# When the second pair of gated linear recurrence tiles runs: beside the chunks of the delta-rule recurrence, in buffers of its own

## What is computed

```python
proj = h @ w_in
pa, xb, gb = jnp.split(proj, (A_PROJ, A_PROJ + B_WIDTH), axis=-1)
ya = rwkv7_time_mix(pa, ...)                       # delta-rule recurrence, 8 heads of 64
yb = rglru_mix(xb, gb, ...)                        # gated linear recurrence, 512 channels
return jnp.concatenate([ya, yb], axis=-1) @ w_out

# rglru_mix
xc = conv_b + sum(xp[:, i:i + seqlen] * conv_w[i] for i in range(4))
r = sigmoid(blocks(xc) @ gate_a_w + gate_a_b)
i_g = sigmoid(blocks(xc) @ gate_x_w + gate_x_b)
log_a = -8.0 * r * softplus(-lam)
u = sqrt(-expm1(2.0 * log_a)) * i_g * xc
h_t = exp(log_a)_t * h_(t-1) + u_t
yb = h * gelu(gb)
```

## Time and profile before

| | |
|---|---|
| median of three runs | 3627.5 us (3625.55 to 3630.48) |
| the profiled execution | 3622.88 us |
| its span, first to last instruction | 3621.2 us |
| TensorE busy | 3446.0 us (95%), 20308 matmuls |
| VectorE, ScalarE busy | 1943.7 us (54%), 1330.2 us (37%) |
| granted TensorE clock, mean | 0.973 |
| instruction queue q8 | 160 packets, 2.62 MB |

### The profile page before, as it was taken

How to read it: one execution, slowest core, us unless ns; L and a number is a source line. 1 busy time by engine, 2 the same in 40 slices (tenths; PEclk the granted TensorE clock), 3 DMA queues, 4 the chain that set the end, 5 groups by cost and what they waited for, 6 DMA issues and landing times.

```text
span 3621.2 us, 47103 instructions
## 1 busy us (share of the span) xinstructions
PE 3446.0 (95%) x20308; PEld 2741.7 (76%) x20308; DVE 1943.7 (54%) x2721; ACT 1330.2 (37%) x1958; POOL 4.0 (0%) x18
## 2 busy tenths in 40 slices
PE   8999896799999999989999999999999999989998
PEld 6888665778888788877578887766788877668886
DVE  5554576456553654243445433566766455766644
ACT  4332454133322423233543322244444233544433
POOL 0000000000000000000000000000000000000000
PEclk9999996899999999999999999999999999999999
DMA  5444330014444342222012222310232231012321
GB/s 182 144 140 146 121 111 20 4 65 140 140 145 143 125 137 96 99 79 87 1 53 99 98 95 102 119 59 24 74 107 99 96 137 59 30 57 95 99 99 58
DMA packets 93087, 342.41 MB, mean 95 GB/s; under 512 B 10320, under 2 KB 10960, under 8 KB 92368
## 3 DMA queue, kind: packets, MB, share of 16 engines
q1 hardware_dynamic: 92880, 339.40, 28.1%
HBM read 337.26 MB, written 2.10 MB: 94 GB/s over the span
## 4 chain that ended last, share of the span: by engine, by line
PE 86%; DVE 7%; ACT 5%; issue 1%; DMA 0%; SPq 0%; DVEq 0%; ACTq 0%
PE ps L755 21%; PE ps L756 20%; PE ps L757 20%; PE ps L772 3%; PE ps L773 3%; PE ps L776 3%; PE ps L795 1%; PE ps L796 1%; PE ps L797 1%; PE ps L1127 1%; DVE SPL L1901 1%; PE ps L1137 1%; ACT SPH L1369 1%; ACT WK L1805 1%; DVE WK L2565 1%
## 5 line engine op out<-in xcount | busy, mean ns | idle before, releaser
L1901 DVE TENSOR_TENSOR SPL<-RAW,SPH 128x1024 fp32r<-128x1024 f32 x522 | 636.7, 1224 | 1066.8 <-ACT SPH L1369 1066.7
L755 PE MATMUL ps<-HH,SPH 128*128 128x512 f32 x2352 | 929.4, 395 | 15.7 <-DVE SPL L1901 6.2
L1369 ACT ACTIVATE SPH<-RAW 128x1024 fp32r<-128x1024 f32 x522 | 548.1, 1056 | 1075.1 <-PE ps L757 957.9
L756 PE MATMUL ps<-HL,SPH 128*128 128x512 f32 x2352 | 918.3, 390 | 0.0
L757 PE MATMUL ps<-HH,SPL 128*128 128x512 f32 x2352 | 918.0, 390 | 0.0
L755 PEld LDWEIGHTS ps<-HH,SPH 128*128 128x128 f32 x2352 | 443.3, 188 | 121.3 <-issue 10.5
L756 PEld LDWEIGHTS ps<-HL,SPH 128*128 128x128 f32 x2352 | 443.6, 189 | 94.7 <-issue 4.0
L757 PEld LDWEIGHTS ps<-HH,SPL 128*128 128x128 f32 x2352 | 443.3, 188 | 93.2
L755 PE MATMUL ps<-AH,SPH 128*128 128x512 f32 x1152 | 449.7, 390 | 0.0
L757 PE MATMUL ps<-AH,SPL 128*128 128x512 f32 x1152 | 448.3, 389 | 0.0
L756 PE MATMUL ps<-AL,SPH 128*128 128x512 f32 x1056 | 410.8, 389 | 0.0
(11 more groups left out here) (430 smaller groups left out, 3575.1 us busy)
## 6 DMA issues: line engine op xcount, KB each, us to landing
RAW<-in_ws SPq DMA_DIRECT2D x522, 512.0 KB, 3.3
RAW<-in_wa SPq DMA_DIRECT2D x96, 512.0 KB, 3.3
WK<-in_sm SPq DMA_DIRECT2D x2, 2784.0 KB, 10.5
WK<-in_cst SPq DMA_DIRECT2D x2, 1664.0 KB, 6.8
X<-in_x SPq DMA_DIRECT2D x8, 256.0 KB, 7.9
out<-X SPq DMA_DIRECT2D x8, 256.0 KB, 2.0
WK<-in_sm SPq DMA_DIRECT2D x1, 768.0 KB, 5.4
PCT<-in_pc SPq DMA_DIRECT2D x1, 349.0 KB, 3.0
```

What stands on the lines that cost most here:

```text
L755: e.matmul(out, wh, rhs[0], start=start, stop=False)
L756: e.matmul(out, wh, rhs[1], start=False, stop=False)
L1369: e.activation(SPH[:, q:q + 1024], RAW[:, r:r + 1024], ACT.Copy).then_inc(hi_ready.did(("hi", n)))
L1901: e.tensor_tensor(SPL[:, q:q + 1024], RAW[:, r:r + 1024], SPH[:, q:q + 1024].bitcast(F32), ALU.subtract).then_inc(lo_ready.did(("lo", n)))
```

## The change

Parts 1 to 4 of tiles 2 and 3 leave the first inverse and stand beside chunks 0 and 1, a tile after the other (`LRU_CHUNK_AT`); part 0 stands one step later than before. The two tiles get other buffers: A and M2 in the last tiles of HH and HL, which they share (so tile 3 waits in part 1 for the scan of tile 2), U in tiles of their own. The last results (part 4) of both are taken after tile 3 is done, since they overwrite those buffers. The chunks wait for `("ml", 5)` only.

```diff
 LRU_AT = {0: [(0, 0), (1, 0)], 1: [(0, 1), (1, 1)], 2: [(0, 2), (1, 2)], 3: [(0, 3), (1, 3)],
-          4: [(0, 4), (1, 4), (2, 0), (3, 0)], 5: [(2, 1), (3, 1)], 6: [(2, 2), (3, 2)], 7: [(2, 3), (3, 3)],
-          8: [(2, 4), (3, 4)]}
+          4: [(0, 4), (1, 4)], 5: [(2, 0), (3, 0)]}
+
+LRU_CHUNK_AT = {(0, 1): [(2, 1)], (0, 3): [(2, 2)], (0, 5): [(2, 3)], (0, 6): [(3, 1)], (1, 0): [(3, 2)],
+                (1, 1): [(3, 3)], (1, 3): [(2, 4), (3, 4)]}
...
             if c and 0 < i <= STEPS_NORM:
                 yield "norm", c - 1, i - 1
+            for j, part in LRU_CHUNK_AT.get((c, i), ()):
+                yield "lru", j, part
...
+        YLc, _ = place("YLc", 2 * T, at=h_at + 14 * T * 4)
...
-        lru_places = [{"M2": wk(26), "A": wk(27), "U": wk(12)}, {"M2": wk(28), "A": wk(29), "U": RS[:]}]
+        lru_places = [{"M2": wk(26), "A": wk(27), "U": wk(12)}, {"M2": wk(28), "A": wk(29), "U": RS[:]},
+                      {"M2": YLc[:, T:2 * T], "A": Yh[:, 7 * T:8 * T], "U": YLc[:, 0:T]},
+                      {"M2": YLc[:, T:2 * T], "A": Yh[:, 7 * T:8 * T], "U": Yh[:, 6 * T:7 * T]}]
...
-                        w.wait_ge(("pe0", 14 + j), ("pe0", 21), ("prep_dd",), *([("ml", 2 + j)] if j >= 2 else []))
+                        w.wait_ge(("pe0", 14 + j), ("pe0", 21), ("prep_dd",), ("proj", s, 21))
...
-                        w.wait_ge(("ga", j), ("halved_b",))
+                        w.wait_ge(("ga", j), ("halved_b",), *([("h_", 2)] if j == 3 else []))
...
-                        w.wait_ge(("yb", j), ("proj", s, 21))
+                        w.wait_ge(("yb", 3 if j == 2 else j), ("proj", s, 21))
```

More of the change, by code:

```diff
@@ L588, in plan_mix0 @@
                     chunk(c, i)
+                elif what == "lru":
+                    lru(c, i)
                 else:
@@ L1506, in lru @@
                 def lru(j, part):
-                    L = lru_places[j % 2]
+                    L = lru_places[j]
                     if part == 0:
@@ L1567, in chunk @@
                         for name, dst, done in (("ktp", rwkv["KT"], "kt"), ("btp", rwkv["BT"], "bt")):
-                            w.wait_ge((name, c), ("prep_dd",), *([("yp", c - 1)] if c else [("ml", 7)]))
+                            w.wait_ge((name, c), ("prep_dd",), *([("yp", c - 1)] if c else [("ml", 5)]))
                             e.activation(dst, ps[name, c][:], ACT.Copy).then_inc(act_done.did((done, c)))
@@ L1578, in chunk @@
                     elif i == 6:
-                        w.wait_ge(("yp", c), *([("ylo", c - 2)] if c >= 2 else [("ml", 7)]))
+                        w.wait_ge(("yp", c), *([("ylo", c - 2)] if c >= 2 else [("ml", 5)]))
                         e.activation(rwkv["Y"][c % 2], ps["yp", c][:], ACT.Copy).then_inc(act_done.did(("yc", c)))
@@ L2187, in chunk @@
                         for hf in range(2):
-                            w.wait_ge((name, c), *([("yp", c - 1)] if c else [("ml", 7)]))
+                            w.wait_ge((name, c), *([("yp", c - 1)] if c else [("ml", 5)]))
                             e.tensor_tensor(v4(MX[name, hf]), v4(ps[name, c, hf][:]), bc4(strict if i == 0 else incl),
```

2 lines of the change are left out of this document (1 added, 1 removed).

## The result

| | before | changed |
|---|---|---|
| median, thirteen runs of each | 3627.5 us (3616.6 to 3635.1) | 3619.2 us (3613.9 to 3623.4) |
| ratio changed to before, 95% | | 0.9978 (0.9970 to 0.9987) |
| the profiled execution, its span | 3622.9, 3621.2 us | 3613.9, 3612.2 us |

The changed kernel ran in two more series: 3621.4 against 3626.1 us (0.9989, 0.9979 to 0.9999) and 3622.7 against 3626.7 us (0.9994, 0.9985 to 1.0002). The mean of the three ratios is 0.9987, or **4.7 us faster**; the first series, with 8.3 us, was its best, and in the third the interval takes in no change at all. The forecast was 1.3 us faster. Single runs of one kernel lie up to 18.5 us apart, so this is a case in which the profile's stretches say more than the medians.

A forecast was written before the change was run, and what follows sets the result against it. Instruction fetch, about 3.65 us per 128 small matmuls, was taken to bound the inverse. Terms -4.1 + 0.1 + 0.2 + 0.8 + 1.7 = -1.3 us gave 3626.2 us from the median 3627.5, range 3619 to 3633.

The forecast's parts named there:

- What paces the inverse: First inverse, chunks 0 and 1: instruction fetch sets about 3.65 us per 128 matmuls; moving the work out gains 4.1 us.
- Rival B: First inverse: waits for VectorE and ScalarE pace it, so 12.2 us come off, -8.8 in all, about 3619 us; chance 0.10.
- The step from the level-3 mask: First inverse: the convolution delays the mask, so its products start at 600.45 and their block fills 0.6 us late.
- Step (1, 1): Tile 3's part 3, 2.6 us of VectorE before level-4 additions of chunks 2 and 3: cost 1.7 us, between 0 and 2.6.
- a further 0.8 us: Level-4 additions of chunks 2 and 3: already late by the 0.8 us that tile 3's gate matmuls cost at (0, 6).
- Steps (0, 1) and (0, 6): Gate matmuls of tiles 2 and 3 beside the chunks: 0.1 us plus 0.2 for instructions at (0, 1), 0.8 at (0, 6).
- The stop at 681.55: Small products behind tile 3's gate matmuls: this 0.97 us instruction stop would fall under the new matmuls and be gone.
- The 0.2 for 1/16 of a block: Step (0, 1): tile 2's 8 gate matmuls take 1/16 of an instruction block from those that follow, costing 0.2 us.
- Rival C: Step (0, 5): VectorE blocked behind ScalarE for tile 2 beyond 2.7 us of cover; +0 to +2 in all, 3629 us; chance 0.14.
- rival D: After 694 us: the clock stays at 1.2 GHz; from 12 us of large matmuls +8, 3634 us; chance 0.10.
- Its sign of being wrong, a clock after 694 us below 1: Trace after the change: a granted clock below 1 after 694 us would show the prediction wrong.
- the clock "adds to this": Large matmuls from 627 to 695 us: -5.5 if all at 2.4 GHz, +5 if 1.2 GHz lasts longer; neither expected.

The follow-up runs named there:

- E3: Changed kernel with the 32x32 products of levels 1 to 4 of the first inverse issued twice; inverse 60.04 us, ratio to before 1.0023.
- E4: Changed kernel with six more unused VectorE operations of 128x512 after step 7 of the first inverse; inverse 46.72 us, ratio to before 0.9991.
- E6: E5 with the 16 gate matmuls of tiles 2 and 3 also issued after step 5, results unused; inverse 49.46 us, ratio to before 1.0016.
- E5: Changed kernel with the convolution of tiles 2 and 3 after step 4, not step 5; inverse 45.81 us, ratio to before 0.9981.
- E7: Changed kernel with tile 3's scan (part 3) moved from step (1, 1) to (1, 2); level-4 additions 7.79 us, ratio to before 0.9990.
- E2: Changed kernel with only the gate matmuls of parts 1 to 3 of tiles 2 and 3 kept; ratio to before 0.9991.
- before again: The kernel before, without an edit, profiled and timed once more; inverse 49.80 us, chunk 1 25.04 us, ratio to before 0.9995.
- E1: Changed kernel with parts 1 to 3 of tiles 2 and 3 left out; chunk 1 25.08 us, ratio to before 1.0009.

## Why the prediction came out as it did

**What paces the inverse: right, and shown.** The forecast was 4.1 us, the mean of the profiles says 4.3. E3 raised the number of blocks by four and paid 3.4 to 3.6 us for each. E4 gave VectorE its work back and paid 0.6. E6 gave TensorE its long products back and paid 3.65. Rival B, by which all of the 12.2 us of removed work would have come off, has fallen, though the first series' 8.3 us is close to its 8.8: its total came near by accident, its mechanism was not at work (E3, E4). With it falls, for this stage, the rule of "Runtime: NRT & Kernel Launch" (Instruction fetch mechanics) in the Trainium skill that block crossings are mostly hidden.

**The step from the level-3 mask (0.6 us late): it did not show.** Behind the moved convolution TensorE waits 1.85, 2.12 and 1.84 us for the mask L2171 in the three profiles (0.61 us for the same mask before; the longest waits for L2171, 2.5 to 3.4 us, are for the mask of level 2, which the change does not touch). But the two blocks around this wait are not longer than others:

```profile
594.50:597.31 2.81, 0.96 (x52) 0.50 0.02 6
597.31:601.41 4.10, 2.98 (x206) 0.50 0.01 4
```

That is 6.91 us for two blocks, and 7.2 in each of the other two profiles, where the prediction had 7.85 (597.35 to 605.2, with the 0.6 in it). The wait took the place of the "issue" wait. E5, which removes the cause, is accordingly no shorter.

**Step (1, 1), 1.7 us: right**, measured 1.56 (E7), at the place and through the additions that it named. That holds at a clock of 1.00: five profiles with the scan against the first one of before, E2 and E7. Whether they were late by a further 0.8 us already, "to L4" can't show.

**Steps (0, 1) and (0, 6), 0.1, 0.2 and 0.8 us: too small for "to L4", where unedited kernels spread by 4.5 us.** TensorE's rows say more. Tile 2's gate products take 1.93 us in each of the three profiles and leave a wait of 0.68 or 0.69 us, 2.6 together, where the wait alone was 2.55 us in the earlier trace rows and 1.73 in the second profile of before: they lie under the wait, as forecast. For tile 3, the stretch from the first record of the step to the end of the L915 behind it (L905 before) was 7.6 and 7.5 us before and 8.3, 7.6 and 7.6 after: the 0.8 shows in one of three. The stop at 681.55 did go, but came back within L915 for 1.85 us. The 0.2 for 1/16 of a block was not measured.

**Rival C, VectorE behind ScalarE: not seen.** In the changed kernel the masks behind tile 2's scan were done at 670.0 us, and their products (L971) began at 671.9, behind the gate products of tile 3. The cover held. For tile 3's square root, ScalarE's table load of 1.28 us ran while the input was still being made, so it cost nothing there:

```profile
676.31 1.28 ACT L1546 ACT_TABLE_LOAD   x1
680.36 0.63 ACT L1546 ACTIVATE YLc<-YLc 128x512 f32<-128x512 f32 x1 [2.77 <-DVE YLc L2116]
```

**The clock: the size was named, the side was not.** The prediction saw that 1.2 GHz after 694 us would cost about +8, gave it to the changed kernel as rival D, and took the clock of before as given. Its sign of being wrong, a clock after 694 us below 1, did come in the changed kernel (1.2 GHz until 697.1 us, chunk 1 at 0.90 and 18.68 us against 17.36), but cost 1.3 us and not 8. The clock did stay low there, for some 7 us of loss, in four of the five profiles of kernels without the scan at (1, 1) (before again, E1, E2, E7) and in none of the eight with it. If the two groups were alike, a split of this kind would come up about once in 140; but I chose the split after seeing it, and nothing was run that sets the clock alone. Its direction is that of the result: with the mixer's own terms at -4.3 and +1.6, that is -2.7, the measured -4.7 leaves 2 us, and a loss of 7 us in a part of the runs of before would be of that size. The mean clocks of the timed runs point the same way: 0.9725 and 0.9728 for the changed kernel where the kernel before beside it had 0.9718 both times, and 0.9735 in the first series. By the 2.8 to 2.9 us per 0.001 above, an estimate, that is 2 and 3 us, uncertain by about 1 each. In which stage it lies, the means don't say, and why a scan on VectorE should change it is open.

**The total.** 3626.2 was forecast and 3619.2 measured in the first series, 0.2 us inside the range, which is luck; 3621.4 and 3622.7 in the next. No measurable change was forecast as the likeliest outcome (0.77), and 0.9978 to 0.9994 is near to that. The weakest step is the one in which the clock "adds to this" with no value: of the missing 3.4 us (4.7 less 1.3), 0.3 are mis-sizes of the two large terms (4.3 for 4.1, 1.6 for 1.7), up to 1.1 are the three small costs, as far as they were nothing, and 2 or more are what the mixer's terms do not account for, most likely the clock, which is argued and not shown.

**A better version.** E5 (0.9981) lies within the 0.9978 to 0.9994 of the changed kernel, which was not timed in its group. No version is measurably faster than the changed kernel.

## What to carry to other kernels

Where a stage is made of very small matmuls, as here, cut the trace at the ends of the "issue" waits and count the instructions between them: if the count is constant, add up the stage as its number of instruction blocks plus the long instructions that have few records; work on other engines beside it was nearly free here (0.6 us for 5 in E4), as it fell into the blocks' slack. Move such long instructions to where TensorE is bound by execution, and the short VectorE operations away from the point where a chain of small additions decides. And profile the same kernel two or three times before explaining a few microseconds: here one unedited kernel had an 8.7 us longer mixer in its second profile than in its first.

## What the runs showed of the hardware that was not expected

- **The clock has a price that depends on when it is low.** Chunk 1 took 17.4 to 18.7 us at a granted clock of 0.90 to 1.00 and 25.0 to 25.1 us at 0.66, with the same matmuls and TensorE busy 97% of the latter. The kernel with half of the recurrence left out (E1) was slower than the full one, its runs at a lower mean clock.
- **A stop for instructions did not vanish under long work here, it moved:** 0.97 us at 681.55 became 1.85 us at 674.72, seven microseconds earlier and in another group.
